# First expert queries in two steps, output turns in halves, and another key order in a six-layer kernel

## The reference

```python
def first_block(x, ...):
    for layer in range(2):
        mix = _diff_attention(...) if layer == 0 else _stick_breaking(...)
        x = _layer_norm(ALPHA * x + mix, ln_g[layer, 0], ln_b[layer, 0])
        ffn = _peer(x, peer_w_q[layer], peer_sub_keys[layer], peer_u[layer], peer_v[layer])
        x = _layer_norm(ALPHA * x + ffn, ln_g[layer, 1], ln_b[layer, 1])

def _peer(x, ...):    # 8 heads; per head a token chooses 16 of 16384 experts
    # queries = x @ w_q; scores of two halves against 128 sub-keys each; 16 best of each half,
    # 16 best of their 256 sums; gates = softmax
    h = gelu(einsum('td,ted->te', xblk, u[ids]))
    return einsum('te,ted->td', gates * h, v[ids])

def second_block(x, ...):
    for i in range(4):               # mixers: dsa (selected), swa (window), mla (latent), dsa
        x = x + mixer(rms_norm(x, norm_mix[i]))
        x = x + sqrelu_mlp(rms_norm(x, norm_mlp[i]), w_up[i], w_down[i])

def dsa_mixer(h, ...):
    q, k, v, q_idx, k_idx, w_idx = split_cols(h @ w_in, ...)
    score = einsum('bqh,bqhs->bqs', w_idx, relu(q_idx . k_idx))   # causal
    sel = top_k(score, 64)           # attention of 16 heads over the selected keys, with a bias
```

## Time and profile before

| | us |
|---|---|
| median of three runs | 2851.61 |
| lowest, highest | 2849.09, 2851.61 |
| profiled execution | 2853.91 |
| its span | 2852.1 |
| TensorE busy | 2529.7 (89%) |
| VectorE busy | 1747.7 (61%) |
| ScalarE busy | 963.0 (34%) |
| GpSimd busy | 642.8 (23%) |
| mean granted TensorE clock | 0.972 |

### The profile page before, as it was taken

How to read it: one execution, slowest core, us unless ns; L and a number is a source line. 1 busy time by engine, 2 the same in 40 slices (tenths; PEclk the granted TensorE clock), 3 DMA queues, 4 the chain that set the end, 5 groups by cost and what they waited for, 6 DMA issues and landing times.

```text
span 2852.1 us, 29296 instructions
## 1 busy us (share of the span) xinstructions
PE 2529.7 (89%) x9773; PEld 1566.7 (55%) x9773; DVE 1747.7 (61%) x3961; ACT 963.0 (34%) x2010; POOL 642.8 (23%) x625
## 2 busy tenths in 40 slices
PE   9888777799887899887877899999999899998999
PEld 3563222255443465443322356885688568875787
DVE  3557667756657766767776456654565556645654
ACT  1412122224322354222221234442444344423543
POOL 0014444433334433434444201002000000002000
PEclk9999999999999999998999999999999989999999
DMA  8139999999999999999999722544154315533352
GB/s 312 61 129 421 421 421 421 420 414 421 396 421 422 418 404 368 421 414 422 420 421 421 323 118 76 205 154 185 41 210 162 145 46 184 190 128 118 133 191 103
DMA packets 110480, 791.63 MB, mean 278 GB/s; under 512 B 12995, under 2 KB 15638, under 8 KB 19478
## 3 DMA queue, kind: packets, MB, share of 16 engines
q0 software_dynamic: 73760, 536.93, 45.6%
q1 hardware_dynamic: 36598, 253.21, 23.7%
HBM read 789.02 MB, written 1.07 MB: 277 GB/s over the span
## 4 chain that ended last, share of the span: by engine, by line
PE 64%; DMA 23%; DVE 7%; issue 3%; ACT 2%; POOL 1%; DVEq 0%; SPq 0%; ACTq 0%; POOLq 0%
DMA weights<-in_peer_uv,scratch 17%; PE psum L1206 14%; PE psum L988 13%; PE psum L1312 12%; PE psum L1269 7%; DMA arena<-in_peer_uv,scratch 6%; PE psum L1271 4%; PE psum L1061 3%; DVE heads_arena L2123 2%; PE psum L1069 2%; PE psum L973 2%; PE psum L1047 1%; PE psum L998 1%; PE psum L1036 1%; PE psum L1025 1%
## 5 line engine op out<-in xcount | busy, mean ns | idle before, releaser
L1206 PE MATMUL psum<-weights,scratch 128*128 128x512 f32 x1224 | 597.1, 627 | 153.3 <-ACT scratch L1611 153.3
L1206 PEld LDWEIGHTS psum<-weights,scratch 128*128 128x128 f32 x1224 | 232.2, 198 | 485.1 <-issue 246.4
L1206 PE MATMUL psum<-arena,scratch 128*128 128x512 f32 x824 | 399.9, 621 | 90.7 <-ACT scratch L1611 90.7
L2578 POOL DMA_INDIRECT weights<-in_peer_uv,scratch x306 | 342.3, 1118 | 494.3 <-PE psum L1206 468.3
L988 PE MATMUL psum<-weights,xT 128*128 128x512 f32 (+2 forms) x920 | 394.1, 585 | 13.7 <-DMA weights<-in_w_qkv_a 6.6
L2392 DVE TENSOR_TENSOR piece<-weights,piece 128x2048 fp32r<-128x2048 f32 x128 | 292.1, 2292 | 181.6 <-ACT piece L1704 181.6
L1312 PE MATMUL psum<-piece,hidden 128*128 128x512 f32 x1536 | 358.9, 390 | 0.0
L1603 ACT ACTIVATE scratch<-scratch 128x2 f32<-128x2 f32 x256 | 52.0, 203 | 884.7 <-DVE heads_arena L2123 884.4
L2578 POOL DMA_INDIRECT arena<-in_peer_uv,scratch x206 | 234.8, 1140 | 462.5 <-PE psum L1206 330.1
L1206 PEld LDWEIGHTS psum<-arena,scratch 128*128 128x128 f32 x824 | 155.8, 196 | 309.2 <-issue 163.0
L1269 PE MATMUL psum<-split_x,piece 128*128 128x512 f32 x896 | 318.6, 398 | 0.0
(11 more groups left out here) (230 smaller groups left out, 2814.4 us busy)
## 6 DMA issues: line engine op xcount, KB each, us to landing
weights<-in_w_up SPq DMA_DIRECT2D x64, 1024.0 KB, 4.9
weights<-in_w_down SPq DMA_DIRECT2D x64, 1024.0 KB, 4.8
weights<-in_w_kv_b SPq DMA_DIRECT2D x16, 1024.0 KB, 9.0
weights<-in_a_w_in SPq DMA_DIRECT2D x6, 2048.0 KB, 10.4
weights<-in_w_qkv_a SPq DMA_DIRECT2D x5, 2048.0 KB, 15.8
weights<-in_w_q_b SPq DMA_DIRECT2D x8, 1024.0 KB, 9.6
weights<-in_w_o_b SPq DMA_DIRECT2D x8, 1024.0 KB, 9.3
weights<-in_peer_w_q SPq DMA_DIRECT2D x8, 1024.0 KB, 9.3
```

The costliest lines, as they stand in the source:

```text
L1206: mm = pe.matmul(psum[g.bank][:, :], diagonal[:, n % DIAGONALS, :], row[:, D + half * BANK:D + (half + 1) * BANK], start=(k == 0), stop=(k ...
L2578: pool.indirect_dma_start(gathered[n % GATHER_SLOTS], None, rows, bass.IndirectOffsetOnAxis(ap=expert[:, w % NT, k:k + 1], axis=0), elemen ...
```

## The change

It has three parts. In the first, TensorE makes the queries and scores of heads 0 to 3 of tile 0, then tile 1's second output half, then the queries and scores of heads 4 to 7; ScalarE's order follows. In the second, a new function `attended_out` replaces the turns and the first output half of both tiles: the first four transposes wait for the first eight heads only, and the other four stand between k = 1 and k = 2 of the projection. ScalarE's and VectorE's order is as it was there. In the third, in the selected layers, TensorE projects `in1[3]` between the key transposes of tile 0 and its index scores; ScalarE copies `in1[3]` and takes root `k1` ahead of the relus of tile 0; VectorE makes tile 1's keys ahead of tile 0's index sum and selection.

```diff
-            def project(blocks, block0=0, turned=None, source=xT, in_parts=False):
+            def project(blocks, block0=0, turned=None, source=xT, in_parts=False, second_half=None):
...
                     for k in range(c.rows):
+                        if second_half and k == KB // 4:
+                            second_half()
                         if n == 0 and turned and k % 4 == 0:
                             copied(turned[k // 4])
...
                 copied(p.x_turn[0].last)
-                for n in range(NT):
-                    query_chunk(p.q, 0, n)
+                query_chunk(p.q, 0, 0)
                 pe.wait_ge(keys_loaded, 16)
-                copied(p.q.groups[0][-1])
-                scores_of(p.s[0])
+                copied(p.q.groups[0][0])
+                scores_of(p.s[0][0:2])
+                project(diff_out.blocks[1][1:2])
+                query_chunk(p.q, 0, 1)
+                copied(p.q.groups[0][1])
+                scores_of(p.s[0][2:4], 4)
...
                 project(l.in1[2], turned=l.x_turn[1].done)
-                turn_prepared(l.key_turn[0], l.k_ready[0])
+                pe.wait_ge(prepared.sem, l.k_ready[0] + 1)
+                turns(l.key_turn[0])
+                project(l.in1[3])
+                copied(l.key_turn[0].last)
                 index_scores(l.index[0])
-                project(l.in1[3])
                 pe.wait_ge(prepared.sem, l.q_ready[0] + 1)
...
+            def attended_out(l, t):
+
+                groups = l.att.v[t * HEADS // l.att.per:(t + 1) * HEADS // l.att.per]
+
+                def second_half():
+                    copied(groups[1])
+                    turns(l.out_turn[t], 1, 2)
+
+                copied(groups[0])
+                turns(l.out_turn[t], 0, 1)
+                project(l.out_blocks[t][0:1], turned=l.out_turn[t].done, second_half=second_half)
...
                 attend(l.att, kind, 0, HEADS)
-                copied(l.att.v[HEADS // l.att.per - 1])
-                turns(l.out_turn[0])
-                project(l.out_blocks[0][0:1], turned=l.out_turn[0].done)
+                attended_out(l, 0)
...
                 attend(l.att, kind, HEADS, NT * HEADS)
-                copied(l.att.v[-1])
-                turns(l.out_turn[1])
-                project(l.out_blocks[1][0:1], turned=l.out_turn[1].done)
+                attended_out(l, 1)
...
             first_queries(peer0)
-            project(diff_out.blocks[1][1:2])
             experts()
...
                 turns(p.x_turn[0])
-                for n in range(2):
-                    queries(0, n)
-                scores_of(p.s[0], 0)
+                queries(0, 0)
+                scores_of(p.s[0][0:2], 0)
                 gate(0, 0)
                 root(ln_root[0, 1], 1)
+                queries(0, 1)
+                scores_of(p.s[0][2:4], 0, 4)
                 turns(p.x_turn[1])
...
                 keys_apart(l.key_turn[0].groups[-1], 0, 2, 1)
+                outputs(l.in1[3], to_y)
+                root(l.root["k1"], 1)
                 relus(l.index[0])
-                outputs(l.in1[3], to_y)
                 turns(l.turn[0])
                 outputs(l.in1[0], to_y)
-                root(l.root["k1"], 1)
...
                 selected_keys(l, 0)
+                selected_keys(l, 1)
                 index_sum(l.index[0])
                 select(0)
-                selected_keys(l, 1)
                 index_sum(l.index[1])
```

More of the change, by code:

```diff
@@ L1185, in second_queries, with scores_of @@
                     scores_of(p.s[1])
-            def scores_of(groups):
+            def scores_of(groups, head0=0):
                 for b, g in enumerate(groups):
@@ L1190, in scores_of @@
                     for j in range(4):
-                        h, c = b // 2 * 4 + j, b % 2
+                        h, c = head0 + b // 2 * 4 + j, b % 2
                         mm = pe.matmul(psum[g.bank][:, j * P:(j + 1) * P], peer_qT[c * HD:(c + 1) * HD, h, :],
@@ L1557, in stick_piece, with scores_of @@
                 last.then_inc(psum_freed[g.bank], 1)
-            def scores_of(groups, t):
+            def scores_of(groups, t, head0=0):
                 for b, g in enumerate(groups):
                     filled(g)
-                    at = (b % 2 * PEER_HEADS + b // 2 * 4) * PEER_KEYS
+                    at = (b % 2 * PEER_HEADS + head0 + b // 2 * 4) * PEER_KEYS
                     act.activation(scores[:, t, at:at + BANK], psum[g.bank][:, :], ACT.Copy)\
```

## The result

The changed kernel takes 2829.3 us (median of six, 2824.4 to 2838.2) against 2851.6 for the kernel before (2847.7 to 2851.8): ratio 0.9925, 95% interval 0.9911 to 0.9940. That is 22.3 us less where 18.2 were forecast (2833.4). The profiled execution took 2825.58 us with a span of 2823.8, at a mean granted clock of 0.981 (before: 2853.91, 2852.1, 0.972). A later series of six gave 2834.3. Over both series the twelve times have a median of 2833.2, and they lie in two clusters, 2824.4 to 2826.9 (four) and 2831.7 to 2838.3 (eight). Where the gap comes from is the main thing that the traces added.

The account below looks back on a forecast made before the run. Gathers filling the DMA engines bound about 190 to 1620 us, then chains of engines waiting in turn. Terms -7.2 - 6.3 - 4.7 = -18.2 gave 2833.4 us from a median of 2851.61; eight times in ten 2823.5 to 2843.

Parts of the forecast that it names:

- Part A: First expert queries: scores follow the first query chunk directly, so the gather stream starts earlier; -7.2 us, bounds -6.5 and -8.5.
- Rival (4): Gather stream: a stall at gathers 5 or 8 takes back the earlier start; 2840.5 us, chance 0.06.
- rival (5): Gather stream runs at a lower rate through 1430 us; 1.3% less costs 18.6 us and wipes out all; chance 0.06.
- Part C: Selected layers 0 and 3: TensorE's wait for tile 1's keys goes; -6.3 us, bounds -5 and -7.5.
- The term at the front: Selected layers, tile 0's index scores: copy hidden, but relus wait behind root k1; -0.2 us each, layer 0 bounds -1.1 and +0.8.
- Part B: Split output turns, eight places: seven at -0.75, plus masks, layer 2 and clock; -4.7 us, bounds +4 and -15.
- masks, +0.4: Layers 0 and 3, tile 0: later selection for tile 1 only narrowly beats attention; 0.2 us left for each.
- layer 2, tile 0, +2.7: Output place at low clock: ScalarE's second copy delays the root, so TensorE waits for rotated heads; +2.7 instead of -0.75 us.
- clock, -2.5: Output places of layer 0 tile 0 and layer 1 both tiles: half of 5.1 us of low-clock cost goes; -2.5 us.
- rival (2): Layers 0 and 1, output places: all three clock falls go, another -2.6 us; 2830.8 us, chance 0.10.
- Rival (1): Layer 2 stays at full clock in tile 0's attention, together 10 us less; 2823 us, chance 0.14.
- Rival (3): Layers 0 and 3: low-clock projections make the root 3.3 us late, holding up attention; about +9, 2842 us, chance 0.14.

Follow-up runs that it names:

- relus' move: Changed kernel with ScalarE doing tile 0's relus ahead of root k1 in the two selected layers: 2825.80 us, ratio 0.9915.
- part two alone: Kernel before with only the split output turns, in all eight places: 2846.13 us, ratio 0.9978.
- after: First series and trace of the changed kernel, all three parts against the kernel before: 2829.3 us, ratio 0.9925.
- after again: The same changed kernel measured once more, with a second trace, against the kernel before: 2834.34 us, ratio 0.9941.
- one and three alone: Two kernels, each the kernel before with one addition: the reordered first queries, 2844.56 us; the new key order in the selected layers, 2845.93 us.

## Why the prediction was right, step by step

**Part A, booked -7.2:** -7.16 within the trace, and the mean start of the gathers is 188.6 in three traces without the part and 181.1 in eleven with it. Gather 8 came at 198.04 (near 199 forecast), tile 1's transposes at 188.55 (189.0). Rival (4) and rival (5) are out: first to last gather takes 1413.6 to 1414.8 us without the part and 1411.6 to 1416.5 with it.

**Part C, booked -6.3:** input to attention means 65.4 (three traces without) and 62.0 (nine with, without the relus' move) in layer 0, 73.7 and 70.8 in layer 3: -3.4 and -3.0, where -3.5 and -2.8 were booked. At the undisturbed clock layer 3 gives 72.80 to 70.42, 2.4. The term at the front was wrong in sign: instead of -0.2 the critical step behind it came 0.5 us later in layer 0 and 0.1 in layer 3 relative to the step before. The bound +0.8 held it, and the cause is the one named, ScalarE's root ahead of the relus. What the prediction did not have is the fall of the clock behind that wait, 1.7 us in five of nine traces of layer 0 and two of nine of layer 3; the means hold it.

**Part B, booked -4.7:** the eight output places sum to 212.7 us in the mean of three traces without the part and 208.4 in four with it (part two alone, after, after again, relus first): -4.3. Its terms:
- seven places at -0.75: measured -0.8 in five, and -1.0 in layer 1, tile 1. Layer 1's tile 0 had the clock's fall in every trace without the part, so its own term can't be told apart.
- masks, +0.4: nothing. Layer 0's and 3's output t0 drop by the full 0.8.
- layer 2, tile 0, +2.7: the mechanism was right, the size too small. It is +4.1 at the low clock (part two alone against one and three alone), up to +4.8 in the second trace of the changed kernel. The step that failed let the transposes of the rotated heads follow at full clock as before (3.66 us); they now follow a wait of 2.4 to 3.2 us, and in four of five traces the clock falls behind it and they take 5.15 to 5.37. In the fifth they take 3.70 and the place 38.55, 2.4 to 3.1 us more than whole, which is near the 2.7 booked. With the attention at the full clock TensorE waits 3.18 us and the place takes 37.70, still more than the 35.4 of the whole turn at the low clock: the place loses.
- clock, -2.5 as half of 5.1: the falls of the six other places had cost about 2.3 us a trace without the part (1.06 + 1.24, 1.15 + 1.24, 1.23 + 1.07 above 30.93 and 19.77) besides layer 1's tile 0, and all of those are gone; layer 1's tile 0 keeps its fall in ten of eleven traces (32.6 to 33.4 with the part, 30.74 in the only trace without a fall). So the half was right in size, and rival (2), that all three falls go, did not come true: two went, the costliest stayed.

**Rival (1), 0.14:** its condition came true in the profiled execution, and with it one of the prediction's own signs of being wrong, layer 2's projection at full clock. Its price was only in part right. It booked 10 us, 5 for the attention and the rest for an output place that turns from a loss to a gain. Between the two traces of the changed kernel the input and attention give 5.9 us, and the output place 2.5, since it loses at the full clock too. That the execution took 2825.6, near the rival's 2823, is partly luck: 2.9 us of it are the fall of the clock in the expert part. The argument against the rival, that part B changes nothing ahead of that attention, was sound: the clock there differs between executions of the same kernel. In the changed kernel it was full in one trace of two, and four times of twelve lie in the fast cluster. A chance near a third would have been better; the prediction took one trace's level for the kernel's.

**Rival (3):** the selected layers' projections ran at full clock and nothing was held up; it is out.

So the total of -18.2 against -22.3 for the first six times, and 2833.2 over all twelve, is no cancelling of large errors: three parts, each within 0.5 us of its sum in the means of the traces, and a scatter of the clock that the first median happened to catch on its fast side. Within part B the masks' 0.4 too much and layer 2's 1.1 too little (+3.8 in the mean of the same four traces, for +2.7) have opposite signs, so its sum is better than its terms.

## What to carry to other kernels

When a copy is split so that its second half waits inside the next product, look at what stands behind it in the copying engine's order: moving the root ahead of the second copy was worth 3.5 to 4.2 us in one place, and the split 0.8 to 1.0 in each of six others. A wait on the matmul engine can cost twice, once itself and once by the clock behind it (3.18 us, then 1.7 for 32 transposes); so book both, or look for the order without the wait. A term for the clock needs several traces of the same kernel; one trace's level is one draw. Plain products in the longest wait did not hold the clock here; it fell behind the next one, the wait for the attention's first exp, and with products there too it did not, in one trace.

## What was not expected of the hardware

- The clock fell at the start of an attention behind waits of 0.95, 1.12 and 2.55 us only, with small products and transposes between them (windows above: 1.00, 0.83, 0.50), and in the changed kernel's first trace it recovered before the same work (0.50 in 2256 to 2260, 0.89 in 2260 to 2264, then 1.00). Six wide products ahead didn't prevent the fall in either of their two traces (short in the second); with two in the last wait there was none, in the one trace taken.
- Transposes follow the granted clock like products: 32 take 3.66 to 3.70 us at the upper level and up to 6.45 at the lower (the changed kernel's second trace, ahead of layer 2's attention), four take 0.61 and 1.06. The Trainium skill, "TensorE: Matmul & The Clock Gate", section "Part 4: PE-mode transpose", says that the full clock does not engage for them; these rows speak against that, while whether they count as activity no run here tells apart.
- ScalarE's root starts 1.29 us after its table load does, and the load is 1.28 long. The Trainium skill, "ScalarE: Activation LUTs", section "What ACT_TABLE_LOAD costs", adds about 1.38 us of draining to such a switch; none shows here.
- Before the first gather, the same instructions differ by up to 1.5 us between executions (180.5 to 182.0 in the eleven traces with part one).
